# The first stage of a fused transformer kernel, taken feature tile by feature tile, with part of its weight splitting on GpSimd

## What is computed

```python
cs = silu(c)                                  # c: one vector of 1024
mod = cs @ ada_w + ada_b                      # ada_w: 1024 x 6144; six vectors of 1024
shift1, scale1, gate1, shift2, scale2, gate2 = split(mod, 6)
h = rmsnorm(x, norm1_g) * (1 + scale1) + shift1
proj = h @ w_in                               # 1024 x 4352
qa, ka, va, qb, kb, vb, ga, gb = split(proj)  # two attention branches, values, two gates
ya = windowed attention of (qa, ka, va); yb = block attention of (qb, kb, vb)
x = x + gate1 * ((sigmoid(ga) * (ya @ w_branch_a) + sigmoid(gb) * (yb @ w_branch_b)) @ w_out)
```

## Time and profile before

| | before |
|---|---|
| median of three runs | 1333.67 us |
| profiled execution, its own time | 1333.61 us |
| span of the core in it | 1332.3 us |
| PE busy | 1253.9 us, 94% |
| DVE busy | 896.0 us, 67% |
| ACT busy | 622.8 us, 47% |
| POOL busy | 189.8 us, 14% |
| chain that ended last | PE 83%, DVE 11%, ACT 2%, POOL 1% |
| first real matmul | 43.18 us after the start |

### The profile page before, as it was taken

The page is one execution under the profiler, slowest core; times in us unless marked ns, Lnnn a source line. Parts: engine busy times, 40 slices in busy tenths (PEclk is TensorE's granted clock), DMA queues, the critical chain, the costliest instruction groups (busy, mean ns, idle before and its releaser), DMA issues.

```text
span 1332.3 us, 23738 instructions
## 1 busy us (share of the span) xinstructions
PE 1253.9 (94%) x9926; PEld 1223.9 (92%) x9926; DVE 896.0 (67%) x1253; ACT 622.8 (47%) x955; POOL 189.8 (14%) x188
## 2 busy tenths in 40 slices
PE   1799998999999999999799999989999999999996
PEld 1798898999999999999699999989999987999996
DVE  7748878867555876655966666676665675866653
ACT  1435544666434444444544454444444455644531
POOL 4004433200122100002400001120000230000022
PEclk9999999999999999999799999989999999999998
DMA  8675556465565355565155555545556531565540
GB/s 332 236 277 184 199 203 238 160 238 211 201 200 181 127 192 186 165 202 174 42 179 167 183 172 163 178 150 179 189 190 206 174 115 60 174 190 190 188 145 32
DMA packets 66978, 238.87 MB, mean 179 GB/s; under 512 B 7286, under 2 KB 9512, under 8 KB 66872
## 3 DMA queue, kind: packets, MB, share of 16 engines
q1 hardware_dynamic: 66280, 235.17, 52.7%
q0 software_dynamic: 592, 2.19, 0.5%
HBM read 236.26 MB, written 1.07 MB: 178 GB/s over the span
## 4 chain that ended last, share of the span: by engine, by line
PE 83%; DVE 11%; ACT 2%; issue 2%; POOL 1%; DMA 0%; SPq 0%; DVEq 0%; ACTq 0%
PE G L543 26%; PE G L544 26%; PE G L545 25%; DVE sb_wlo L1274 2%; PE G L563 1%; DVE sb_sig L1297 1%; DVE sb_rstd L1318 1%; ACT sb_whi L961 1%; PE G L579 1%; PE A L618 1%; DMA sb_raw<-in_wstream 0%; DVE sb_xl L1764 0%; ACT sb_p L1237 0%; PE A L641 0%; DVE sb_X L1627 0%
## 5 line engine op out<-in xcount | busy, mean ns | idle before, releaser
L1274 DVE TENSOR_TENSOR sb_wlo<-sb_raw,sb_whi 128x1024 fp32r<-128x1024 f32 x395 | 488.2, 1269 | 95.0 <-ACT sb_whi L961 94.9
L543 PE MATMUL G<-sb_xh,sb_whi 128*128 128x256 f32 (+2 forms) x1868 | 535.4, 287 | 17.4 <-DVE sb_gu L1552 7.5
L544 PE MATMUL G<-sb_xl,sb_whi 128*128 128x256 f32 (+2 forms) x1868 | 533.3, 286 | 0.0
L545 PE MATMUL G<-sb_xh,sb_wlo 128*128 128x256 f32 (+2 forms) x1868 | 532.0, 285 | 0.0
L961 ACT ACTIVATE sb_whi<-sb_raw 128x1024 fp32r<-128x1024 f32 x395 | 404.4, 1050 | 186.1 <-PE G L545 174.3
L543 PEld LDWEIGHTS G<-sb_xh,sb_whi 128*128 128x128 f32 x1868 | 356.3, 191 | 22.4 <-DVE sb_gu L1552 8.3
L544 PEld LDWEIGHTS G<-sb_xl,sb_whi 128*128 128x128 f32 x1868 | 355.7, 190 | 0.1
L545 PEld LDWEIGHTS G<-sb_xh,sb_wlo 128*128 128x128 f32 x1868 | 355.6, 190 | 0.0
L543 PE MATMUL G<-sb_hh,sb_whi 128*128 128x256 f32 (+1 forms) x1056 | 301.1, 285 | 6.5 <-DVE sb_X L1326 4.3
L545 PE MATMUL G<-sb_hh,sb_wlo 128*128 128x256 f32 (+1 forms) x1056 | 301.5, 285 | 0.0
L544 PE MATMUL G<-sb_hl,sb_whi 128*128 128x256 f32 (+1 forms) x992 | 283.1, 285 | 0.0
(11 more groups left out here) (272 smaller groups left out, 1110.0 us busy)
## 6 DMA issues: line engine op xcount, KB each, us to landing
sb_raw<-in_wstream SPq DMA_DIRECT2D x443, 512.0 KB, 4.4
sb_bias<-bias_scratch POOLq DMA_DIRECT2D x1, 2048.0 KB, 17.0
sb_X<-in_xT SPq DMA_DIRECT2D x1, 1024.0 KB, 5.7
out_T<-sb_X SPq DMA_DIRECT2D x4, 256.0 KB, 2.2
sb_con<-in_consts SPq DMA_DIRECT2D x1, 632.0 KB, 6.9
sb_vec<-in_vecs SPq DMA_DIRECT2D x1, 82.5 KB, 2.0
sb_X<-in_metaT POOLq DMA_DIRECT2D x1, 64.0 KB, 4.8
sb_boh<-in_bias_oh SPq DMA_DIRECT2D x1, 51.0 KB
```

Source lines behind the costliest of these rows:

```text
L543: e.matmul(out, w_h, xs, start=k0 + s.kt == 0, stop=False)
L544: e.matmul(out, w_h, xr, start=False, stop=False)
L545: m = e.matmul(out, w_l, xs, start=False, stop=k0 + s.kt == ktotal - 1)
L1274: e.tensor_tensor(wlo[:, i % NSPLIT, 0:w], raw[:, c % NRAW, 0:w], f(whi[:, i % NSPLIT, 0:w]), ALU.subtract).then_inc(lo_done, 1)
```

## The change

The stream is reordered so that the first stage works feature tile by feature tile. For each feature tile kt, two chunks of `ada_w` (`ada_h{kt}_0`, `ada_h{kt}_1`) hold the scale and shift columns of that tile for all eight row groups; behind them come the query/key chunks, now ordered feature tile first (thirteen blocks each). The number of chunks is the same. x is loaded in two halves behind the first two chunks.

- `mod` for one tile: eight products of 128x256 in one accumulator, the first on ScalarE, seven on VectorE, each waiting for the one before; TensorE sums them into two columns of `A0`; VectorE makes gain and shift with two small operations.
- The squares of x move from GpSimd to ScalarE (four operations of 128x512); TensorE adds them up by eight matmuls into the mean.
- GpSimd makes y = x * rstd, one tile at a time; ScalarE makes `tmp` = y * gain + shift and rounds it to `xh`; VectorE `xl` = tmp - xh.
- The thirteen output tiles accumulate together in seven banks (`G0`, `G1`, `A1` to `A3`) over the eight feature tiles, and leave at the end: four copies on ScalarE, three on VectorE.
- GpSimd makes the low halves of the chunks 2, 5, 7 and 10 of the thirteen (`POOL_LO`), between its y tiles.
- `va` goes to bank `A0`; two pieces of `ada_w` for gate1 lie ahead of it, two behind. GpSimd reads the bias table back after its last low half.

```diff
+QK_TILES = 13
+QK_BANKS = ((0,), (1, 2), (3, 4), (5, 6), (7, 8), (9, 10), (11, 12))
+POOL_LO = (2, 5, 7, 10)
+QK_NEEDED = [(QK_TILES * (kt + 1) - 1) // CH for kt in range(KT)]
...
+    for kt in range(KT + 2):
+        if kt < KT:
+            for half in range(2):
+                group(f"ada_h{kt}_{half}", [("ada_w", 0, _r(r * P), _r((i * KT + kt) * P)) for r in _r(4 * half, 4) for i in (1, 0)], True)
+        while kt >= 2 and done * CH < QK_TILES * (kt - 1):
+            group(f"qk_{done}", qk[done * CH:(done + 1) * CH], True)
+            done += 1
...
 # TensorE
+            for kt in range(KT):
+                if kt < KT - 2:
+                    shift_scale_sum(kt + 2)
                 e.wait_ge(xl_done, XSTAGE["h"] + kt + 1)
+                for s in steps["qk"][QK_TILES * kt:QK_TILES * (kt + 1)]:
+                    if s.opens:
+                        low_half(e, s.i)
...
 # ScalarE
+            for kt in range(KT):
+                if kt < KT - 2:
+                    first_product(kt + 2)
+                split_hi(QK_NEEDED[kt])
+                e.wait_ge(y_done, kt + 1)
+                e.wait_ge(gain1_done, 2 * kt + 2)
+                if kt >= 2:
+                    e.wait_ge(xl_done, kt - 1)
+                e.activation(tmp[:, kt % 2, 0:SEQ], sig[:, KT + kt, :], ACT.Identity, bias=mod[:, kt:kt + 1], scale=g1m[:, kt:kt + 1]).then_inc(f_done, 1)
+                e.wait_ge(f_done, kt + 1)
+                e.activation(xh[:, kt, COLS1], tmp[:, kt % 2, 0:SEQ], ACT.Copy).then_inc(xh_done, 1)
...
 # VectorE
+            def shift_scale_products(kt):
...
+                        if r > 1:
+                            e.wait_ge(acc1_done, 7 * kt + r - 1)
+                        w = raw[:, c % NRAW, r % 4 * 2 * P:(r % 4 + 1) * 2 * P]
+                        e.scalar_tensor_tensor(acc1(kt), w, csil[:, r:r + 1], acc1(kt), ALU.mult, ALU.add).then_inc(acc1_done, 1)
+            def shift_scale(kt):
+                e.wait_ge(sum1_done, kt + 1)
+                e.tensor_scalar(g1m[:, kt:kt + 1], A[0][:, 0:1], b1[:, kt:kt + 1], V("norm1_g", kt), ALU.add, ALU.mult).then_inc(gain1_done, 1)
+                e.tensor_tensor(mod[:, kt:kt + 1], A[0][:, 1:2], V("ada_b", kt), ALU.add).then_inc(gain1_done, 1)
+            shift_scale_products(0)
+            shift_scale_products(1)
+            rstd_from("norm1", rstd, root, COLS1)
+            shift_scale(0)
+            for kt in range(KT):
+                if kt < KT - 2:
+                    shift_scale_products(kt + 2)
+                if kt < KT - 1:
+                    shift_scale(kt + 1)
+                split_lo(QK_NEEDED[kt])
+                e.wait_ge(xh_done, kt + 1)
+                e.tensor_tensor(xl[:, kt, COLS1], tmp[:, kt % 2, 0:SEQ], f(xh[:, kt, COLS1]), ALU.subtract).then_inc(xl_done, 1)
...
 # GpSimd
-            e.wait_ge(x_in, 16)
-            for kt in range(KT):
-                square(X[:, kt, COLS1], kt == 0, COLS1)
...
+            e.wait_ge(rstd_done, RSTD["norm1"])
+            for kt in range(KT):
+                e.tensor_tensor(sig[:, KT + kt, :], X[:, kt, COLS1], rstd[:, COLS1], ALU.mult).then_inc(y_done, 1)
+                if kt % 2:
+                    i = POOL_LO[kt // 2]
+                    c, w = plan.split[i], len(chunks[plan.split[i]]) * P
+                    e.wait_ge(hi_done, i + 1)
+                    e.tensor_tensor(wlo[:, i % NSPLIT, 0:w], raw[:, c % NRAW, 0:w], f(whi[:, i % NSPLIT, 0:w]), ALU.subtract).then_inc(lo_pool, 1)
             e.wait_ge(rows_out, 16)
-            e.wait_ge(left_act, plan.left_act["qk1"])
             e.dma_start(bias[:, :, :], hankel).then_inc(bias_in, 16)
```

More of the change, by code:

```diff
@@ L177, in weight_plan @@
             chunks[-1].append(b)
+    where["qk"] = [place for i in range(QK_CHUNKS) for place in where.pop(f"qk_{i}")]
     return chunks, where
@@ L254, in gemm_plan @@
 def gemm_plan():
-    out = [(f"qk{i}", 2 if i < 6 else 1, KT) for i in range(7)] + [("va", 1, KT), ("vb", 4, KT)]
+    out = [("qk", QK_TILES, KT), ("va", 1, KT), ("vb", 4, KT)]
     out += [(f"gate{i}", 2, 4) for i in range(HEADS1)] + [(f"bra{i}", 2, 4) for i in range(4)] + [(f"brb{i}", 2, 4) for i in range(4)]
@@ L265, in pair_plan @@
 def pair_plan():
-    out = [("mod0", 0, 1)] + [(f"qk{i}", 1, 1 if i < 6 else 0) for i in range(7)] + [("va", 1, 1), ("vb", 1, 1), ("mod4", 0, 1)]
+    out = [("vb", 1, 1), ("mod4", 0, 1)]
     for i in range(HEADS1 + 2):
@@ L562, in token_major @@
                         for j, (s_, m_) in enumerate(((xs, w_h), (xr, w_h), (xs, w_l))):
[L563 removed]
+                            t = e.matmul(outs[i][0:m, 0:width], s_, m_, start=kt == 0 and j == 0 and not (shared and i), stop=kt == nk - 1 and j == 2, skip_group_check=shared)
                     if last.closes or kt == nk - 1:
@@ L580, in mod_sum, with shift_scale_sum @@
                 m.then_inc(mod_summed, 1)
-            e.wait_ge(consts_set, 5)
-            mean(0, COLS1, "x")
-            mod_sum("mod0", 0, 4)
+            def shift_scale_sum(kt):
+                e.wait_ge(acc1_done, 7 * kt + 7)
+                if kt:
+                    e.wait_ge(gain1_done, 2 * kt)
+                else:
+                    e.wait_ge(root_done, ROOT["norm1"])
+                for n in range(2):
+                    m = e.matmul(A[0][:, n:n + 1], acc1(kt)[:, n * P:(n + 1) * P], one_col[:, 0:1], start=True, stop=True)
+                m.then_inc(sum1_done, 1)
@@ new lines, in tensor_program @@
+            e.wait_ge(consts_set, 5)
+            for kt in range(KT):
+                if kt % 2 == 0:
+                    e.wait_ge(xsq_done, kt // 2 + 1)
+                m = e.matmul(A[0][:, 0:SEQ], mean_ones[:, 0, :], sig[:, kt, :], start=kt == 0, stop=kt == KT - 1)
+            m.then_inc(mean_done, 1)
+            e.wait_ge(rows_in, 32)
+            e.matmul(A[1][0:HEADS1, 0:BIASC], brow[:, :], boh[:, :], start=True, stop=True).then_inc(bias_made, 1)
+            for kt in range(2):
+                shift_scale_sum(kt)
@@ L598, in tensor_program @@
-            vsrc = lambda kt, a, m: (xh[:, kt, META + a:META + a + m], xl[:, kt, META + a:META + a + m])
-            for name, w in (("va", P), ("vb", 4 * P)):
-                g = pair(name)
-                token_major(name, w, KT, vsrc, [(0, P), (P, P)], [g[:, 0, :], g[:, 1, :]])
+                if kt == 0:
+                    e.wait_ge(bias_row, 1)
+                for s in steps["qk"][QK_TILES * kt:QK_TILES * (kt + 1)]:
+                    if s.opens:
+                        low_half(e, s.i)
+                    w_h, w_l = (w[:, s.i % NSPLIT, s.off * P:(s.off + 1) * P] for w in (whi, wlo))
+                    out = qk_out[s.t]
+                    e.matmul(out, w_h, xh[:, kt, COLS1], start=kt == 0 and s.t in qk_first, stop=False, skip_group_check=True)
+                    e.matmul(out, w_h, xl[:, kt, COLS1], start=False, stop=False, skip_group_check=True)
+                    m = e.matmul(out, w_l, xh[:, kt, COLS1], start=False, stop=kt == KT - 1, skip_group_check=True)
+                    if s.closes or s.j == QK_TILES * KT - 1:
+                        m.then_inc(mm_done, 1)
@@ L1380, in vector_program @@
+            for part in (0, 1):
+                ada_piece(4, part)
+            split_lo(plan.lo_to[steps["va"][0].i])
+            e.wait_ge(mm_done, ended["qk"])
+            for i in (1, 3, 5):
+                qk_copy(i)
+            splits("va")
+            for part in (2, 3):
+                ada_piece(4, part)
+            splits("vb")
+            e.wait_ge(mm_done, ended["vb"])
+            e.tensor_copy(vtok[:, 1, P:5 * P], G[plan.pair["vb"]][:, 1, :]).then_inc(left_dve, 1)
             mod_out("mod4")
```

202 lines of the change are left out of this document (101 added, 101 removed).

## The result

The median after the change was 1324.4 us over eight runs (1318.77 to 1331.58), against 1333.97 us for the kernel before on the same chip. The ratio is 0.992 (95% interval 0.989 to 0.994), so the change saves 0.8%. The profiled execution took 1328.38 us and has a span of 1327.0 us.

What follows compares the result with a forecast made beforehand. VectorE was taken to bound the kernel up to 43 us, with TensorE queued behind. Query/key matmuls ending at 76.6 instead of 83.54 gave -6.9 us on 1333.61, so 1326.8 us for the median, range 1318 to 1333.

Steps and rivals of the forecast that it cites:

- The bound, and the place of the gain: First stage: VectorE bounds it up to 43 us with TensorE queued behind; gain lies before TensorE's first real matmul at 43.18.
- E: Time at which the query/key matmuls end: 83.54 us before the change, predicted 76.6 after it.
- The start: Stage up to the third feature tile's products on VectorE: predicted to start at 18.0 us (17.2 to 19).
- Turn 0: VectorE's first turn: 6.65 us plus 0.8 for y tiles and 1.65 for GpSimd's chunk 2, 9.1 in all.
- Turns 1 to 5: VectorE's next five turns: 5.51 us each, 27.55 together, plus 2.5 for y tiles and 4.95 for chunks 5, 7, 10.
- The prices in it: VectorE costs: chained product 0.51 us, xl 0.45, gain and shift 0.35, y tile 0.41, low half on GpSimd 1.65.
- TensorE's rest: After xl of tile 5: three TensorE turns, 13.7 us, plus 0.8 for a possible low clock, ending at 76.6.
- Behind it: After the query/key matmuls: no added cost; low halves and bias table in time, heads as before but shifted.
- the rival on the hand-overs: Query/key turns: costlier chained products and late high halves or sums give back 4.5 us: 1331.2 us, chance 0.22.
- The border of 0.5%: Whole kernel: 6.7 us is distinguishable from no change, border 1327.0; faster given 0.45, same 0.47.
- GpSimd is not hidden: Denies the first-stage rival that GpSimd does not hold VectorE up: gain 17 us, time 1316.5, chance 0.12.
- The slower case: Query/key turns: TensorE's waits keep it at 1.2 GHz, 15 us later than before: 1349 us, chance 0.08.

Runs made afterwards that it cites:

- all_dve: Changed kernel with all thirteen low halves on VectorE, none on GpSimd: 1320.95 us, ratio 0.988.
- no_gpsimd: Changed kernel with all low halves on VectorE and no y tiles on GpSimd; ScalarE takes x itself, so h lacks rstd: 1315.5 us, ratio 0.984.
- before_pool_lo3: Kernel before the change, with only the low halves of query/key chunks 5, 7 and 10 moved to GpSimd: 1333.56 us, ratio 1.000.
- before_pool_lo: Kernel before the change, with the low halves of query/key chunks 2, 5, 7 and 10 moved to GpSimd: 1340.65 us, ratio 1.003.
- best: Changed kernel, all low halves on VectorE, six products in two accumulators, two on ScalarE, y tiles spread out, unread matmuls filling four second-attention waits: 1310.76 us, ratio 0.980.

## Why the prediction was right, and where it was right by luck

- *The bound, and the place of the gain.* Right: VectorE, without a wait, sets the pace until `xl` of tile 5, TensorE the end. `all_dve` and `no_gpsimd` move E by what they take off VectorE. One step of it was wrong: TensorE was to wait for `xl` in each of turns 1 to 5, and it waited ahead of tiles 2, 3 and 5 only (1.41, 0.80 and 0.80 us). The low level up to 32.0 us kept it at work until tile 1 was there, and ahead of tile 4 VectorE's turn was its shortest, 5.3 us.
- *The start.* 18.81 instead of 18.0 us. The mean matmuls ended at 15.5, not at 15.0, and ScalarE's first product followed the table load.
- *Turn 0.* 9.5 instead of 9.1 us. *Turns 1 to 5.* 34.7 instead of 35.0 us. `xl` of tile 5 ended at 63.1, predicted 62.1.
- *The prices in it were less good than their sum.* A chained product was 0.52 (0.51 predicted). A low half on GpSimd cost VectorE 2.1 us, not 1.65: 4.50 for two halves instead of 2.35, `xl` 2.58 instead of 0.42, products 5.64 instead of 3.67. That error was 1.8 us in all, near the upper bound of 2.2 that was given. Two others took most of it back. VectorE's own turn is 5.31 us, not 5.51 (turn 4 has nothing of GpSimd beside it), 1.0 us over five turns: an `xl` lets the next operation start after 0.33 and gain and shift take 0.25, not 0.45 and 0.35. And one y tile lay ahead of the products. The turns 0 to 5 took 44.2 us where VectorE's own work is 33.1 (6.53 in `no_gpsimd` and five times 5.31); of the 11.1 us that GpSimd cost, the low halves are about 8.3, and 2.8 are left, 0.40 us for each of seven y tiles, as predicted (0.41), but 0.5 us less in all. The rows also show the form of the loss: VectorE loses nearly the whole of GpSimd's operation.
- *TensorE's rest.* 15.2 instead of 14.5 us: twelve of its matmuls ran at the low level, 1.2 GHz. In the other three profiles with this stage it took 13.9 us. Up to E 46 starts are 0.20 to 0.25 us apart, against the 16 to 24 that I had counted on, but 34 of them lie ahead of `xl` of tile 5, where VectorE sets the pace. With the start the rest makes E 1.7 us later than 76.6 in the first profile; in the others E is 76.3 to 77.0, with 76.6 between them.
- *Behind it.* Right as far as it went: no wait for the bias table, low halves in time, the heads shifted by 5.3 us.
- *The time.* 1326.8 predicted, 1324.4 measured, and 1328.4 in the profiled execution. But the sum was the stage only, -6.9 us, and the stage gave -5.3 in that profile and up to -7.2 in others. The rest is terms that the prediction did not have: -6.0 us from the place of the tensors, 0 to +9.8 us from the second attention stage (about a third of the runs of the kernel before lie on the upper level that I put down to it), and -3.8 us from the rest, 3.2 of it other stretches at the low clock. They cancel in the profile, where -5.3 us is left, and that is luck, as is a median 2.4 us from the forecast. Without the first term the median would stand at about 1330, an estimate from the spacings above, between the forecast and the rival on the hand-overs. The border of 0.5% was passed, against the slightly larger chance that I gave to no change.
- *The rivals.* GpSimd is not hidden (`no_gpsimd`). The slower case had the right ingredient, waits that bring the clock down, but 46 slow matmuls up to E and not three turns more of them. That it could decide 1000 us later, in a stage the change does not touch, was in none of the cases.
- *A part of the change that works against it.* The low halves on GpSimd: 5.2 to 5.4 us of the stage. The same move is free where VectorE is not the bound and the half is not wanted at once (`before_pool_lo3`), and costs 7.5 us of E where it is (`before_pool_lo`).

On GpSimd beside VectorE the runs decide how far the rule cited in the prediction goes. Beside GpSimd's low half VectorE loses 1.97 us (products at 55.69), 2.16 (`xl` at 39.02), 2.14 (its own low halves at 22.98) and 2.20 (the one of `before_pool_lo` at 67.59). The Trainium skill, "SBUF — State Buffer", section "Who interferes with whom", names an exclusive lock on the port pair that the two share, and says that a VectorE instruction with two SBUF inputs contends with a GpSimd instruction that reads SBUF; the trace agrees. It works both ways: in `best` the y tile of GpSimd at 22.30 spans 3.11 us, against 0.72 for the one at 18.30, while VectorE's two low halves beside it take 2.34 us as they do alone. The figure of the Trainium skill, "GPSIMD Engine Reference", section "3.1 Elementwise — side-by-side cycle accounting", led to an estimate of 2.25 us for one such operation. The rows have 2.36 to 2.73 us for it and a loss of 2.1 us on VectorE, so that estimate was nearer than the 1.65 that I took from rows of other shapes.
